# A transformer stack on one core: output stage and feed-forward of depth 0 run for 512 and for 256 tokens one behind the other

## What is computed

```python
mod   = silu(c)     @ w_mod[l] + b_mod[l]     # six vectors for x
mod_c = silu(c_ctx) @ w_mod[l] + b_mod[l]     # six vectors for ctx
y, yc = even_mixer(modulate(x, ...), modulate(ctx, ...), we_in, we_out, ...)   # the last step: [..] @ w_out
x   = x   + gt_m  * rmsnorm(y,  g_post_mix)
h   = modulate(x, g_pre_ffn, sh_f, sc_f)
x   = x   + gt_f  * rmsnorm(swiglu(h,  w_ffn_in, w_ffn_out), g_post_ffn)
ctx = ctx + cgt_m * rmsnorm(yc, g_post_mix)
hc  = modulate(ctx, g_pre_ffn, csh_f, csc_f)
ctx = ctx + cgt_f * rmsnorm(swiglu(hc, w_ffn_in, w_ffn_out), g_post_ffn)
```

## Time and profile before

| | us |
|---|---|
| median of 3 runs (2863.14 to 2871.65) | 2865.51 |
| profiled execution | 2870.03 |
| its span in the trace | 2868.2 |
| PE busy, share | 2779.6, 97% |
| DVE busy | 1581.2, 55% |
| ACT busy | 992.4, 35% |
| POOL busy | 1108.5, 39% |
| DMA | 310.09 MB, mean 108 GB/s |

### The profile page before, as it was taken

The page is one execution under the profiler, slowest core; times in us unless marked ns, Lnnn a source line. Parts: engine busy times, 40 slices in busy tenths (PEclk is TensorE's granted clock), DMA queues, the critical chain, the costliest instruction groups (busy, mean ns, idle before and its releaser), DMA issues.

```text
span 2868.2 us, 41972 instructions
## 1 busy us (share of the span) xinstructions
PE 2779.6 (97%) x15962; PEld 2380.3 (83%) x15962; DVE 1581.2 (55%) x2696; ACT 992.4 (35%) x1732; POOL 1108.5 (39%) x601
## 2 busy tenths in 40 slices
PE   8989999999999999999999999999999999999998
PEld 6778877888888789988888888888877788888887
DVE  6788875555545758745555565555544522422223
ACT  3267231111111447633222332222454843322222
POOL 1333213323323253335454445444433344344443
PEclk8999999999999999999999999999999999999999
DMA  5222523232333022224454335444223233133321
GB/s 233 78 51 79 199 80 127 90 122 80 106 113 96 31 74 60 75 74 150 162 178 155 103 119 178 158 146 161 97 70 100 81 95 95 53 111 99 98 88 59
DMA packets 89736, 310.09 MB, mean 108 GB/s; under 512 B 10881, under 2 KB 13057, under 8 KB 88193
## 3 DMA queue, kind: packets, MB, share of 16 engines
q1 hardware_dynamic: 89602, 308.24, 32.9%
HBM read 287.23 MB, written 2.10 MB: 101 GB/s over the span
## 4 chain that ended last, share of the span: by engine, by line
PE 86%; DVE 8%; ACT 2%; issue 1%; DMA 1%; POOL 1%; SPq 0%; ACTq 0%; DVEq 0%; POOLq 0%
PE ps L323 73%; PE ps L2041 3%; PE ps L2029 2%; PE ps L2011 2%; PE ps L524 1%; PE ps L724 1%; DVE dump L369 1%; DVE negm L2090 1%; PE ps L380 1%; PE ps L2234 1%; PE ps L1825 1%; PE ps L2014 1%; DMA raw<-w_stream 1%; DVE ps L808 0%; ACT prob L2063 0%
## 5 line engine op out<-in xcount | busy, mean ns | idle before, releaser
L300 POOL TENSOR_TENSOR w_lo<-raw,w_hi 128x1024 fp32r<-128x1024 f32 x367 | 936.4, 2560 | 1367.6 <-ACT w_hi L294 1367.6
L294 ACT ACTIVATE w_hi<-raw 128x1024 fp32r<-128x1024 f32 x367 | 383.6, 1057 | 1218.2 <-PE ps L323 1103.7
L323 PE MATMUL ps<-n_hi,w_hi 128*128 128x512 f32 (+1 forms) x1744 | 639.5, 367 | 10.5 <-DVE n_lo L831 9.5
L323 PE MATMUL ps<-n_lo,w_hi 128*128 128x512 f32 (+1 forms) x1744 | 628.0, 360 | 0.0
L323 PE MATMUL ps<-n_hi,w_lo 128*128 128x512 f32 (+1 forms) x1744 | 627.9, 360 | 0.0
L323 PEld LDWEIGHTS ps<-n_hi,w_hi 128*128 128x128 f32 x1744 | 329.4, 189 | 66.8 <-DVE n_lo L831 9.8
L323 PEld LDWEIGHTS ps<-n_lo,w_hi 128*128 128x128 f32 x1744 | 329.6, 189 | 50.9 <-issue 1.9
L323 PEld LDWEIGHTS ps<-n_hi,w_lo 128*128 128x128 f32 x1744 | 329.4, 189 | 49.4
L369 DVE CUSTOM_DVE_ANT_0 dump<-modraw 128x1024 f32<-128x1024 f32 x196 | 346.6, 1769 | 17.2 <-DMA modraw<-mod_stream 11.6
L1266 DVE TENSOR_TENSOR y<-y,ps 128x512 f32<-128x512 f32 x360 | 221.7, 633 | 219.4 <-PE ps L323 219.4
L323 PE MATMUL ps<-ffn_hi,w_hi 128*128 128x512 f32 (+1 forms) x928 | 308.7, 364 | 10.1 <-DVE y L1264 5.4
(11 more groups left out here) (305 smaller groups left out, 3705.8 us busy)
## 6 DMA issues: line engine op xcount, KB each, us to landing
raw<-w_stream SPq DMA_DIRECT2D x367, 512.0 KB, 4.0
modraw<-mod_stream SPq DMA_DIRECT2D x152, 512.0 KB, 3.5
mod_pair<-mod_first SPq DMA_DIRECT2D x7, 1024.0 KB, 12.5
l_qs<-l_q_hi SPq DMA_DIRECT2D x32, 128.0 KB, 2.3
l_qs<-l_q_lo SPq DMA_DIRECT2D x32, 128.0 KB, 2.4
l_qs<-l_q_hi SPq DMA_DIRECT2D x16, 192.0 KB, 2.9
l_qs<-l_q_lo SPq DMA_DIRECT2D x16, 192.0 KB, 3.5
xl<-x_in SPq DMA_DIRECT2D x1, 2048.0 KB, 7.8
```

The lines of the kernel that those rows point to most:

```text
L294: nc.scalar.activation(w_hi[:, c % RING, :], raw[:, c % RING, :], ACT.Copy).then_inc(hi_ready, 1)
L300: nc.gpsimd.tensor_tensor(w_lo[:, c % RING, :], raw[:, c % RING, :], w_hi[:, c % RING, :].bitcast(F32), ALU.subtract).then_inc(lo_ready, 1)
L323: mm = nc.tensor.matmul(out, w[a], x[b][:, off:off + n], start=first and i == 0, stop=last and i == 2)
```

## The change

The output stage is run for x (512 columns, `l0_out`) and then for ctx (256 columns, `l0_outc`), and so is the feed-forward (`l0_ffn`, `l0_ffnc`). `STAGES` has their blocks twice, so 74 more blocks are read and split. The norms of one stream stand beside blocks of the other: x's norms behind its output beside the output blocks of ctx; ctx's two norms beside x's feed-forward; x's norm behind the feed-forward and the one before depth 1 beside ctx's feed-forward; ctx's last two beside the query blocks of depth 1, which now come before key and value blocks. Beside a feed-forward VectorE adds the squares of all chunks first, and TensorE makes one sum (`norm_sum_added`). In groups of ctx's feed-forward VectorE splits the two output blocks' low parts, GpSimd the other four. The matmuls of `keep_warm` go, GpSimd's additions to x go to VectorE, and the feed-forward loops of depth 0 are written out.

The modulation is ordered by a list of blocks with the rows that each is used for: in the output stage 28 chunks for x's row alone; in x's feed-forward 68 blocks, first for ctx's row, later for one row or both, through four slots; in ctx's feed-forward none.

```diff
-STAGES = [("l0_in", 10), ("l0_pool", 1), ("l0_out", 8), ("l0_ffn", FFN_BLOCKS),
+STAGES = [("l0_in", 10), ("l0_pool", 1), ("l0_out", 8), ("l0_outc", 8), ("l0_ffn", FFN_BLOCKS), ("l0_ffnc", FFN_BLOCKS),
...
+ENTRIES = [(c, (0, 1)) for c in range(MOD_FIRST, 20)] + [(c, (0,)) for c in range(20, MOD1)]
+OUT_ENTRIES, FFN_ENTRIES = 4, len(ENTRIES)
+ENTRIES += [(c, (1,)) for c in range(20, 40)]
+_singles = [(c, (1,)) for c in range(40, MOD1)] + [(c, (0,)) for c in range(64, MOD_TAIL)]
+for _i in range(16):
+    ENTRIES += [(MOD1 + _i, (0, 1))] + _singles[2 * _i:2 * _i + 2]
...
+    OUT_MODS = [4, 4, 4, 4, 3, 3, 3, 3]
+    def l0_out_pe(pe, mixed):
         for n in range(KC):
...
+            if n >= 4:
+                pe.wait_ge(OUT_COPIES, n - 3)
...
+                mm = product(w, (h_hi[:, k, :], h_lo[:, k, :]), [(ps[:, n % 4, :], 0, S)], k == 0, k == 7)
             mm.then_inc(w_used, 1)
+            if n >= 3:
+                norm_sum(pe, "x_mix_post", n - 3)
+        norm_sum(pe, "x_mix_post", 5)
+        norm_sum(pe, "x_mix_post", 6)
+        for n in range(KC):
+            c = FIRST["l0_outc"] + n
+            pe.wait_ge(lo_ready, c + 1)
+            pe.wait_ge(OUT_COPIES, 5 + n if n < 2 else KC + n - 1)
+            project(h_hi, h_lo, c, [(ps[:, n % 2, 0:C], S, C)]).then_inc(w_used, 1)
+            if n == 0:
+                norm_sum(pe, "x_mix_post", 7)
+            for k in {2: (0,), 3: (1, 2), 4: (3, 4, 5), 5: (6, 7)}.get(n, ()):
+                norm_sum(pe, "x_ffn_pre", k)
...
+    def split_lo_dve(dve, c):
+        dve.wait_ge(hi_ready, c + 1)
+        dve.wait_ge(lo_ready, c)
+        nc.vector.tensor_tensor(w_lo[:, c % RING, :], raw[:, c % RING, :], w_hi[:, c % RING, :].bitcast(F32),
+                                ALU.subtract).then_inc(lo_ready, 1)
...
         def step(c, d, group):
             g, gd = group[:2]
+            if f["split_on_dve"]:
+                split_lo_dve(dve, c + 4)
             ffn_mult(dve, f, 2 * g + 1, 2 * gd, c, d)
             ffn_hidden_lo(dve, f, 2 * g + 1, 2 * gd)
+            if f["split_on_dve"]:
+                split_lo_dve(dve, c + 5)
             mods(g, 0, group)
...
-        keep_warm(pe, "l0_ffn_pre", 0)
-        norm_pe(pe, "l0_ffn_pre")
-        keep_warm(pe, "l0_ffn_pre", 1)
-        ffn_pe(pe, l0_ffn, last_group_pe)
-        sums_after(pe, "l0_ffn_post")
-        keep_warm(pe, "l1_mix_pre", 0)
-        norm_pe(pe, "l1_mix_pre")
-        keep_warm(pe, "l1_mix_pre", 1)
+        l0_out_pe(pe, l0_in["mix_lo"])
+        ffn_pe(pe, l0_ffn, last_group_pe, lambda pe, g: beside_pe(pe, "c_mix_post", "c_ffn_pre", g))
+        ffn_pe(pe, l0_ffnc, last_group_pe, lambda pe, g: beside_pe(pe, "x_ffn_post", "x_l1_pre", g))
         l1_in_pe(pe, l1_in)
```

More of the change, by code:

```diff
@@ L361, in mod_block @@
[L361 to L370, removed]
+    MOD_ROWS = [rows for _, rows in ENTRIES]
@@ new lines, in load_mod, with mod_block @@
+    def load_mod(sp, p, i=0, n=0):
+        same = [q for q in range(p) if MOD_SLOT[q] == MOD_SLOT[p]]
+        if same:
+            sp.wait_ge(mod_ops, mod_ops_before(same[-1] + 1) + i * n)
+        sp.dma_start(mod_slot(p), A["mod_stream"][bass.ds(p + i * n, 1)].rearrange("o p n -> (o p) n")
+                     ).then_inc(mod_landed[MOD_SLOT[p]], 16)
+    def mod_block(dve, p, outs, where, i=0, n=0, first_row=None):
+        ops = mod_ops_before(p)
+        dve.wait_ge(mod_landed[MOD_SLOT[p]], 16 * (mod_turn(p) + 1) + i * (n // MOD_RING * 16))
+        for j, m in enumerate(mod_rows(p)):
+            dve.wait_ge(mod_ops, ops + j + i * n)
+            row = first_row if m == 0 and first_row is not None else c_rows[:, m, :]
+            if p >= TAIL and tail_chunk(p - TAIL + MOD_TAIL) >= MOD2:
+                row = c2_row
+            nc.vector.tensor_tensor_reduce(where, mod_slot(p), row, 1.0, 0.0,
+                                           ALU.mult, ALU.add, outs[j]).then_inc(mod_ops, 1)
@@ L373, in first_there, with mod_entry @@
+    def mod_entry(dve, p, where, first_row=None):
+        c, rows = ENTRIES[p]
+        dst, first = (modv_a, MOD0) if c < MOD1 else (modv_b, MOD1)
+        mod_block(dve, p, [dst[m][:, c - first:c - first + 1] for m in rows], where, first_row=first_row)
     def first_there(eng, k):
@@ L409, in mod_group @@
     def mod_group(dve, c, count, dst, where, i, n, number):
-        ops, each = mods_of(c)
-        first = MOD1 if c < MOD_TAIL else c - tail_chunk(c) + MOD_TAIL
+        p = TAIL + c - MOD_TAIL
+        first = c - tail_chunk(c) + MOD_TAIL
         dve.wait_ge(mod_copied, number)
         for j in range(count):
[L415 to L418, removed]
@@ L1232, in ffn_dve @@
         ffn_hidden_lo(dve, f, 0, 0)
[L1233 to L1237 removed]
+        if beside:
+            beside(dve, -1, 1)
         def mods(g, part, group):
             if f["mods"]:
+                m0, each, dst = f["mods"]
                 i, count = group[2], each[part]
```

1078 lines of the change are left out of this document (590 added, 488 removed).

## The result

| | before | after |
|---|---|---|
| median of the runs, us | 2868.58 (4 runs, 2863.14 to 2872.55) | 2905.32 (4 runs, 2900.15 to 2909.56) |
| ratio after : before | | 1.0129, 95% interval 1.0102 to 1.0155 |
| profiled execution, its span | 2870.03, 2868.2 | 2906.69, 2904.9 |
| PE busy, share of the span | 2779.6, 97% | 2763.1, 95% |
| mean granted clock of PE | 0.990 | 0.977 |

A forecast was written before the change was run, and what follows sets the result against it. TensorE's columns bound the feed-forward, with norm gaps before and behind it. Stretches of +1.7, -45.7 and +7.2 sum to -36.8 us: profiled 2870.0 becomes 2833, median 2829; own range 2818 to 2840, stated range 2806 to 2856.

The forecast's parts named there:

- Stretch A: Output stage, first output matmul to first feed-forward matmul: from 109.1 to 110.8 us, +1.7.
- 4.8 us a pair: Output stage: time per pair of modulation chunks, 1.27 + 3.55 us for product and slot refill, bounds 4.71 and 5.46.
- modulation keeps up: Rival, output stage: modulation loads land sooner or DVE begins earlier, chain starts at 320, 25 us less, 2804; chance 0.12.
- term of 4 us: Output stage: two blocks and a sum at 1.2 GHz, some 4 us more of PE, half of it behind VectorE.
- Stretch B, x: x's feed-forward: 363.9 us, from 66 x 5.44, two sums, 1 for the start and 3 for VectorE.
- 20.6 of 21.8: x's feed-forward: VectorE needs 20.6 us a group of the 21.8 it has outside the output blocks, so it fits.
- page's mean of 1.77 us a reduction: x's feed-forward: price of each of VectorE's eight modulation products a group, taken from groups with four.
- VectorE beside x is late: Rival, x's feed-forward: nearly each product meets a split, about 2.7 us late x 10, +28, 2857; chance 0.12.
- Stretch B, context: Context's feed-forward: 195.8 us, from 66 x 2.88, 1.7 and 4 for weights.
- the context's weights: Rival, context's feed-forward: block six ready at 15.7 instead of 11.5 us, 4.2 x 11 = +46, 2875; chance 0.08.
- The 4 us put for weights: Context's feed-forward: allowance for late weight splits, between 0 and 27 us.
- Stretch C: Input projections of depth 1: from 80.3 to 87.5 us, +7.2, with 16 sums of 256 columns and 1 for context h.

The follow-up runs named there:

- run 1: Changed kernel with each of the 84 modulation reductions in x's feed-forward cut to 64 of 1024 columns: 2849.47 us in one execution.
- run 2: Changed kernel with GpSimd writing only 64 of 1024 columns of each low part in x's feed-forward: 2854.10 us in one execution.
- run 4: Changed kernel with 25 to 52 warming matmuls of ones at seven places in x's feed-forward where PE waited 3 us or more: 2909.33 us.
- run 5: As run 4, but fillings fitted to the waits: 12 to 27 warming matmuls, behind the first two chunks: 2884.11 us, ratio to before 1.0049.
- run 3: Changed kernel with four slots instead of two for modulation blocks in the output stage: 2883.07 us, ratio to before 1.0058.
- run 6: Changed kernel with four output-stage slots and half of x's feed-forward reductions moved, one behind each of additions 0, 2, 4, 7: 2852.55 us, ratio to before 0.9947.
- run 8: As run 6, reductions behind additions 1, 3, 5, 7, small operations spread, last groups' silu chain ahead of norm work: 2835.41 us, ratio to before 0.9894.
- run 7: As run 6, beside the context: last groups multiply ahead of the norm's last low parts, 12 small operations spread: 2852.48 us, ratio to before 0.9942.

## Why the prediction was wrong, point by point

**Stretch A, +1.7 forecast, +8.3 measured.** The mechanism was right: modulation with one product a block waits for refills, and sums of late copies hold up the context blocks. The term that failed is the 4.8 us a pair, worked out from one row of 3.44. It was 5.5, at the upper bound of 5.46, since a load took 4.3 us (4.0 to 4.2 in runs 1, 2, 4 and 5) where the row had 3.44 from load to product; 14 pairs make 9.8 us, of which the stretch shows 6.6. Part of that is this execution: in the four others with the same output stage a pair took 5.1 to 5.2, and the miss is 2.2 to 3.3. Run 3 shows that four slots take 19 to 24 us out of the stretch, which was the rival "modulation keeps up": its condition never came with two slots. The clock there was 0.83 and 0.87, so it fell as the term of 4 us supposed; how much of the stretch that cost is not shown, since run 3 can't be split into clock and copies.

**Stretch B, x: 363.9 forecast, 413.0 measured.** The step that failed is the check of VectorE's cover, "20.6 of 21.8". Three things were wrong in it. It took the page's mean of 1.77 us a reduction, which came from groups with four; with eight it was 1.99. It left out that everything with two SBUF operands is held up as well, also operations of 0.18 us. These two alone don't explain the miss: with 1.99 the sum is 22.3, still inside 21.8 plus the 2.7 of the output banks. Third, it added up a whole group, although VectorE's work stands in two places, each ahead of a multiplication that PE needs within two blocks; time left over in the output blocks (VectorE idles 51 us there for PE over the stretch) can't be used by work that stands elsewhere. Runs 1 and 2 show the cause, and run 6 and run 8 that the same work in other places fits better: VectorE was never full. It took both, hold-ups and places: run 2 takes away the first, run 8 mends the second, and either way most of the waits go. The named rival "VectorE beside x is late" was the case that came, with a chance of 0.12. Its price was too low. By its own terms 25.6 of 23.1 is 2.5 a group, 25 us and not 28 (and 7 us above 2829 is 2836, not the 2840 of the range; neither slip decides anything), and it counted neither the places nor the clock: 35 of waits and some 13 of slow matmuls (run 5).

**The clock.** I charged it in stretch A alone. Waits of 1.5 us in groups 4 and 5 left it at 1.00; behind those of 3 us and more it fell. In later runs it fell behind most waits of 2.0 to 2.4 us too (0.95 from 700 to 736 in run 8, behind one of 2.1). The Trainium skill ("TensorE: Matmul & The Clock Gate", section "Why this matters for your kernels") asks for no idle gaps between bursts. Here the traces agree, with a stretch that is 14 us shorter in run 5, but for another place than the one where I weighed the rule: not where the change removed warming matmuls, but where it made new waits.

**Stretch B, context: 195.8 forecast, 209.9 measured.** Splits in the order of the ring were no trouble (waits of 0.46 and 0.79 in eleven groups), so the rival on the other side, the context's weights, was wrong: that its 2875 is the nearest of the rivals' times to 2905 says nothing for it. The 4 us put for weights came to 1.3. What came instead was 3.53 behind small operations in group 1 and 4.53 in the last group, with the clock behind both (0.83 from 840 to 850, 0.76 from 1000 to 1014), and a group took 17.51 between silus instead of 17.28. The end of a feed-forward exposes the chain silu, multiplication, high, low. The change has two such ends where there was one, and the sum had none. Most of the 4.41 and 4.53 was order and not the chain itself: run 1 leaves 1.1 of the first, and run 8 leaves 2.1 and 2.2.

**Stretch C**, 87.5 forecast, 87.0 measured: right. **The rest**: unchanged to 0.3 us. The prices of PE were right too: 5.44 us a block (run 1: 363.2 for 66 blocks, sums and start) and, within 1.5%, 2.88 (by the 17.51 above). At these prices nothing is left that the written-out loops could have cost.

**The first 4.4 us** are not the change's. The first matmul on h comes at 54.7 to 55.4 us in six profiled executions (before, runs 1, 2, 5, 6, 8) and at 57.9 to 58.6 in four (after, runs 3, 4, 7). All ten have the same 418 instructions ahead of it. What makes the difference stays open.

That run 8, at 2835.4, comes near the forecast of 2829 is luck and no proof of the sum. Its stretch A is 20 us below the forecast, thanks to four slots that the change did not have, and its stretch B, at 578.1, is 18 us above.

## What to carry to other kernels

Check a cover place by place, not as a sum over a group: list what stands in an in-order queue ahead of each instruction that the bounding engine waits for, each at its price under contention, and compare with the time to that wait. An operation of VectorE with two SBUF operands is priced by what GpSimd does in that moment; put it behind GpSimd's last split, or between operations that wait anyway, before you move it to another stage. Where a bounding engine gets new waits, add its slower clock behind each, and where a stage is cut in two, add its exposed end twice (1 to 2 us each here, once the order is right).

## What the runs showed that was not expected

- Two operations of 16 columns took 2.64 us together, and one of 8 columns 2.19, beside splits of 2.4 us; without a split operations of 8 to 24 columns take 0.15 to 0.18. Being small does not protect from the other engine's lock.
- A matmul of plain fp32 operands, 128 columns, is two records and 0.226 us a call, the price of 512 columns of fp32r.
- VectorE's lateness repeats to 0.02 us over executions: the wait in group 1 was 4.33, 4.32, the one ahead of the first sum 6.50, 6.49 in two kernels whose output stages differ by 24 us.
- The start of the program has two lengths, 3 us apart, in executions of the same instructions, and the same output stage took 113.0 to 117.4 us. One profiled execution is thus no measure for a term of a few microseconds.
